# x loaded first, stage changes that wait for the last block but one, compression weights behind the modulation tiles, query rotation in the loop's first steps

## What is computed

```
c_act = silu(c)
mods  = c_act @ ada_w[l] + ada_b[l]            # shift, scale, gate of each norm ("modulation")
x = x + gate * hgrn2(modulate(rms_norm(x)))                    # segments h_q h_f h_v h_g h_out
x = x + gate * swiglu(modulate(rms_norm(x)))                   # ffn0_in / ffn0_out, twice
k, v = compress / select / window of modulate(rms_norm(x))     # n_kvc n_ks n_vs n_kw n_vw
q = rms_norm(per head)(modulate(x) @ w_q); q_rope = rope(q)    # n_q
x = x + gate * attention(q, q_rope, k, v) @ w_out              # attention loop, n_out
x = x + gate * swiglu(...)                                     # ffn1
x = x + diff_attention(rms_norm(x)) @ w_o                      # d_q d_k d_v d_out
x = x + squared_relu_mlp(rms_norm(x))                          # mlp0
x = x + s5(rms_norm(x)); x = x + squared_relu_mlp(...)         # s_glu, mlp1
```

## Time and profile before

| | value |
|---|---|
| median of three runs | 2970.71 us |
| profiled execution, its own time | 2976.58 us |
| its span in the trace | 2974.8 us |
| TensorE busy | 2788.4 us (94%) |
| VectorE busy | 1643.8 us (55%) |
| ScalarE busy | 1059.9 us (36%) |
| mean granted TensorE clock | 0.971 of full |

### The profile page before, as it was taken

One profiled execution on the slowest core, in us unless ns is written; L12 is line 12 of the kernel. 1 busy time (PEld: TensorE's weight loads), 2 busy tenths in 40 slices (PEclk: granted clock), 3 DMA queues, 4 the chain that ended last, 5 costly groups with the idle time before them and its releaser, 6 DMA issues.

```text
span 2974.8 us, 38309 instructions
## 1 busy us (share of the span) xinstructions
PE 2788.4 (94%) x14746; PEld 2238.9 (75%) x14746; DVE 1643.8 (55%) x2350; ACT 1059.9 (36%) x1559; POOL 100.4 (3%) x135
## 2 busy tenths in 40 slices
PE   5999999999979899999999998899999968999999
PEld 4898778888668556788887775788887757778787
DVE  4566566766436776533334557477777394353342
ACT  3312233222323565332233448332341524342231
POOL 2004000000011000000000100000000000000000
PEclk9999999999989999999999999999999988999999
DMA  5640346565363100333333420144444661323232
GB/s 209 199 148 1 105 136 198 149 197 157 105 182 107 43 1 15 97 88 96 94 87 110 126 79 1 57 101 134 141 143 150 231 108 64 92 85 99 85 99 71
DMA packets 402088, 326.36 MB, mean 110 GB/s; under 512 B 14920, under 2 KB 387360, under 8 KB 400928
## 3 DMA queue, kind: packets, MB, share of 16 engines
q1 hardware_dynamic: 319936, 232.80, 26.7%
q10 hardware_dynamic: 77376, 80.07, 8.4%
q0 software_dynamic: 4640, 11.60, 1.5%
HBM read 293.05 MB, written 19.86 MB: 105 GB/s over the span
## 4 chain that ended last, share of the span: by engine, by line
PE 62%; issue 23%; DVE 9%; DMA 3%; ACT 2%; POOL 1%; ACTq 1%; DVEq 0%; POOLq 0%
PE ps L451 44%; PE ps L429 3%; PE ps L445 2%; PE ps L433 1%; DVE ada_acc L1781 1%; DMA ada_ring<-in_ada_w 1%; PE ps L899 1%; DVE ada_ring L513 1%; PE ps L919 1%; PE ps L1649 1%; PE ps L2648 1%; PE ps L887 1%; DVE h_area L1783 1%; DVE h_area L1785 1%; DMA xin<-in_x 1%
## 5 line engine op out<-in xcount | busy, mean ns | idle before, releaser
L451 PE MATMUL ps<-hh,whi 128*128 128x512 f32 x1744 | 693.5, 398 | 5.0 <-DVE xT L2484 1.6
L451 PE MATMUL ps<-hh,wlo 128*128 128x512 f32 x1744 | 681.7, 391 | 0.0
L451 PE MATMUL ps<-hl,whi 128*128 128x512 f32 x1744 | 681.1, 391 | 0.0
L392 DVE TENSOR_TENSOR wlo<-raw,whi 128x2048 fp32r<-128x2048 f32 x198 | 453.9, 2292 | 364.7 <-ACT whi L388 364.7
L388 ACT ACTIVATE whi<-raw 128x2048 fp32r<-128x2048 f32 x198 | 377.6, 1907 | 381.5 <-PE ps L451 250.9
L451 PEld LDWEIGHTS ps<-hh,whi 128*128 128x128 f32 x1744 | 329.1, 189 | 80.0 <-issue 11.9
L451 PEld LDWEIGHTS ps<-hl,whi 128*128 128x128 f32 x1744 | 329.2, 189 | 71.6 <-issue 4.5
L451 PEld LDWEIGHTS ps<-hh,wlo 128*128 128x128 f32 x1744 | 328.8, 189 | 69.7
L451 PE MATMUL ps<-hid_h,whi 128*128 128x512 f32 x756 | 306.7, 406 | 0.0
L451 PE MATMUL ps<-hid_l,whi 128*128 128x512 f32 x756 | 298.4, 395 | 0.0
L451 PE MATMUL ps<-hid_h,wlo 128*128 128x512 f32 x756 | 298.4, 395 | 0.0
(11 more groups left out here) (413 smaller groups left out, 4076.0 us busy)
## 6 DMA issues: line engine op xcount, KB each, us to landing
raw<-in_ffn_w_in SPq DMA_DIRECT2D x44, 1024.0 KB, 6.0
ada_ring<-in_ada_w ACTq DMA_DIRECT2D x82, 512.0 KB, 4.4
raw<-in_ffn_w_up SPq DMA_DIRECT2D x32, 1024.0 KB, 5.3
raw<-in_ffn_w_down SPq DMA_DIRECT2D x32, 1024.0 KB, 5.6
raw<-in_ffn_w_out SPq DMA_DIRECT2D x32, 704.0 KB, 4.5
raw<-in_hgrn_w_in SPq DMA_DIRECT2D x16, 1024.0 KB, 5.6
raw<-in_attn_w_qkv SPq DMA_DIRECT2D x12, 1024.0 KB, 5.1
s_area<-cp_dram SPq DMA_DIRECT2D x6, 2048.0 KB, 9.0
```

What stands on the lines that cost most here:

```text
L392: nc.vector.tensor_tensor(wlo[:, par, :], raw[:, par, :], whi[:, par, :].bitcast(F32), ALU.subtract).then_inc(w_lo, 1)
L451: m = nc.tensor.matmul(ps[:, bank, :], tile(w, kt, j), x[:, kt, :], start=(kt == 0 and n == 0), stop=(kt == k - 1 and n == 2))
```

## The change

x is issued as the first DMA of SyncE's queue. Its squares are taken from the untransposed tiles (`accum_out` gives one sum per token), VectorE spreads the four sums over diagonal matrices, and four short matmuls with ones broadcast them. The folded sums are written in two groups, the scales in bank 4, then the shifts in bank 6, and VectorE adds the shifts (`first_shift`) behind the first two normed tiles, ahead of the first `convert_lo`. All changes of stage use the rule that `need` had. The compression weights are issued behind n_kvc's second block. In the last block of segments in `norm_after`, VectorE evicts ahead of `ada_sums`, and TensorE adds the squares ahead of the last `ada_products`. Query pair 1 moves from nb 8 to nb 9, pair 2 from nb 9 into loop steps 1 to 5, pair 3 from steps 4 to 8 into steps 6 to 10; the reciprocal roots get buffers of their own.

```diff
@@ sync
+            sp.dma_start(xin[:, :, :], a["x"][0].rearrange("(t p) d -> p t d", p=P)).then_inc(x_in, 16)
             for kt in range(FIRST):
@@ scalar
-            act.dma_start(xin[:, :, :], a["x"][0].rearrange("(t p) d -> p t d", p=P)).then_inc(x_in, 16)
...
             for kt in range(KT):
                 act.wait_ge(mm, kt + 1)
-                if kt >= 2:
-                    act.wait_ge(ssq_rdy, kt - 1)
-                nc.scalar.activation(sq[:, kt % 2, :], ps[:, kt % 4, :], ACT.Square).then_inc(sq_rdy, 1)
                 nc.scalar.activation(xT[:, kt, :], ps[:, kt % 4, :], ACT.Copy).then_inc(ev_v, 1)
+                if kt % 2:
+                    t = kt // 2
+                    if t >= 2:
+                        act.wait_ge(x_sq, t - 1)
+                    nc.scalar.activation((sq, xn)[t % 2][:, :, :].rearrange("p s n -> p (s n)"), xin[:, t, :], ACT.Square,
+                                         accum_out=x_ssq[:, t:t + 1]).then_inc(x_sq, 1)
@@ vector, ada_first_dve
+                if kt == 3:
+                    first_square_spread(dve)
+        def first_square_spread(dve):
+            for t in range(TT):
+                dve.wait_ge(x_sq, t + 1)
+                nc.vector.tensor_scalar(rstd[:, t * P:(t + 1) * P], ident[:, :], x_ssq[:, t:t + 1], None, ALU.mult
+                                        ).then_inc(sq_rdy, 2)
@@ tensor
+        def first_square_sums(pe):
+            for t in range(TT):
+                pe.wait_ge(sq_rdy, 2 * t + 2)
+                nc.tensor.matmul(ps[:, 7, t * P:(t + 1) * P], ones[:, :], rstd[:, t * P:(t + 1) * P], start=True, stop=True,
...
-            for j in range(NV):
...
-            m.then_inc(ada0_used, 1)
+            for bank, part in ((4, range(KT, NV)), (6, range(KT))):
...
+                m.then_inc(ada0_used, 1)
@@ scalar
+        def cmp_loads(act):
+            act.dma_start(w1v, a["cmp_w1"][1].rearrange("(m p) n -> p m n", p=P)).then_inc(w1_in, 16)
             act.dma_start(w1k, a["cmp_w1"][0].rearrange("(m p) n -> p m n", p=P)).then_inc(w1_in, 16)
...
         def n_hook_act(act, link, nb):
+            if nb == 1:
+                cmp_loads(act)
@@ vector
-            if nb >= 7:
-                for piece in query_pieces(dve, nb - 7):
+            if nb in (7, 9):
+                for piece in query_pieces(dve, (nb - 7) // 2):
...
-            last_query = query_pieces(dve, 3)
+            last_queries = query_pieces(dve, 2) + query_pieces(dve, 3)
...
-                if 4 <= w < 9:
-                    last_query[w - 4]()
+                if 1 <= w < 11:
+                    last_queries[w - 1]()
@@ vector, linear
+                    late = s.name in norm_after and isinstance(b, int) and b == s.n - 1
+                    if not late:
+                        ada_sums(dve, s, b, par)
                     evac(b, par)
+                    if late:
+                        ada_sums(dve, s, b, par)
@@ tensor, linear
-                if change and need is None:
-                    boundary(pe, s)
-                elif change:
+                if change:
                     if s.ea0 - prev.act > 0:
                         pe.wait_ge(ev_a, s.ea0 - prev.act)
                     pe.wait_ge(ev_v, s.ev0 - prev.dve)
...
-                ada_products(pe, s, s.n - 1, (s.g0 + s.n - 1) % 2)
                 if m is not None:
                     square_sums(s, m, s.n - 1, (s.g0 + s.n - 1) % 2)
+                ada_products(pe, s, s.n - 1, (s.g0 + s.n - 1) % 2)
```

More of the change, by code:

```diff
@@ L557, in ada_first_pe @@
             pe.wait_ge(ada0_sum_v, FIRST)
-            for j in range(NV):
-                m = nc.tensor.matmul(ps[:, 4, j:j + 1], ada_sum[:, j * P:j * P + P], ones[:, 0:1],
-                                     start=False, stop=True, skip_group_check=True)
-            m.then_inc(ada0_used, 1)
+            for bank, part in ((4, range(KT, NV)), (6, range(KT))):
+                for j in part:
+                    m = nc.tensor.matmul(ps[:, bank, j:j + 1], ada_sum[:, j * P:j * P + P], ones[:, 0:1],
+                                         start=(j == 0), stop=True, skip_group_check=True)
+                m.then_inc(ada0_used, 1)
         def ada_bias(dve, s):
@@ L2423, in _, with first_shift @@
             dve.wait_ge(cols_rdy, 1)
[L2424 to L2426 removed]
+            link(nc.vector.tensor_tensor(mods[:, 8:16], ps[:, 4, 8:16], cols_a[:, 8:16], ALU.add))
+            link(modulated_gain(0, ROWS["norm_mix"], 8))
+            def first_shift():
+                dve.wait_ge(ada0_used, FIRST + 2)
+                nc.vector.tensor_tensor(mods[:, 0:8], ps[:, 6, 0:8], cols_a[:, 0:8], ALU.add).then_inc(mods_rdy, 1)
                 convert_lo(dve, segs[0], 0, 0, 0)
@@ L2447, in apply @@
                                                    op0=ALU.mult, op1=ALU.mult).then_inc(xn_rdy, 1)
+                    if j == 0 and kt == 1:
+                        first_shift()
                     if kt:
@@ L2498, in _ @@
             if upto >= 2:
-                dve.wait_ge(mods_rdy, 1)
                 apply(0, 0, *mod_cols(0), FIRST_UNITS)
@@ L2675, in body @@
                     first = isinstance(b, int) and b == 0
-                    if change and need is not None and isinstance(b, int) and b == 1:
+                    if change and isinstance(b, int) and b == 1:
                         boundary(pe, s)
```

61 lines of the change are left out of this document (29 added, 32 removed).

## The result

The changed kernel takes 2947.27 us in the median of four executions (2944.24 to 2949.64), against 2973.28 us for the kernel before beside it (2970.0 to 2978.29): a ratio of 0.9911 with a 95% interval of 0.9892 to 0.9929, that is 26 us less. Its profiled execution took 2947.76 us, its span is 2945.8 us; the span before was 2974.8, so by the two traces the gain is 29.0 us. I had forecast 2931.7 us and 39.0 us of gain, with a range of 2921 to 2943: the gain was forecast too large by half, and the median lies 4 us above the range.

The account below looks back on a forecast made before the run. TensorE, busy 2788.4 of 2974.8 us, was taken as the bound, so only its waits and half clock could give much. Terms -17.3 - 16.2 - 6.5 - 1.9 + 2.9 = -39.0 from 2970.71 gave 2931.7 us, range 2921 to 2943.

Parts of the forecast that it names:

- start: Kernel start: first weight product at 39.7 instead of 57.04, -17.3 us, range -13 to -20.
- stage changes outside n_: At h_v, ffn0_in1, ffn1_in1, mlp1_in1: waits two blocks back are long met; part of -6.5 us, bounds 0 and -8.
- compression weights, with n_vs and n_vw: n_kvc to n_kw: loads moved behind let n_ks start earlier, -16.2 us; n_vs and n_vw waits also go.
- late eviction: Last blocks of h_out and n_out: eviction ahead of the sums, -1.9 us, bounds 0 and -2.5.
- query rotation: Attention loop: carries ten pieces instead of five, +2.9 us; 0 if hidden, +5.7 if nothing is hidden.
- I charge 1.0: Ahead of n_kw: weights ready between 856.4 and 863.4, n_vs covering TensorE until 861.4; 1.0 us charged.
- first rival: n_kw: ScalarE held too long by 4.4 MB of compression weights, TensorE waits 5.9 us plus 2.9 half clock; 2939.5, chance 0.15.
- The first modulation tile: n_kvc: tile issued at 823.6 instead of 836.87, landed at 830.4 instead of 844.2; n_ks starts 14.3 us earlier.
- third rival: Kernel start: the change does nothing, since DMA bounds it in any case; 2949.0 us, chance 0.05.
- second rival: Stage changes: waits only put off to the next block by late eviction or conversion; 2938.2 us, chance 0.08.
- slower rhythm: Attention loop: ten pieces push VectorE behind the exponentials, each of 68 steps keeps a longer turn; 3006 us, chance 0.02.
- signs of being wrong: L530 ending past 34, or ScalarE's L680 issues reaching past n_vs's end, with a gap ahead of n_kw's L451.

Follow-up runs that it names:

- the second trace: The changed kernel run once more without any further change, against the kernel before: 2943.53 us, ratio 0.9898.
- the last version: Changed kernel, old query rotation, tables behind n_kvc's second eviction, SyncE issuing compression loads behind n_kw's weights, w1v behind n_vw's: 2935.16 us, ratio 0.9862.
- the version in two parts: Changed kernel with compression loads split on ScalarE's queue, w1v one block later than the other four: 2943.47 us.

## Why the prediction was wrong, by its own steps

**The size.** Forecast were 39.0 us; the medians show 26.0 in one session and 31.3 in another; the two traces of the changed kernel stand 29.0 and 34.7 us under the one before. Term by term:

| term | forecast | changed kernel's trace |
|---|---|---|
| start | -17.3 | -16.4 |
| stage changes outside n_: h_v, ffn0_in1, ffn1_in1, mlp1_in1 | -4.0 | -4.7 |
| compression weights, with n_vs and n_vw | -16.2 - 2.5 = -18.7 | -13.8 (-12.8 again) |
| late eviction | -1.9 | -1.8 |
| query rotation | +2.9 | +3.2 |
| s5 and diff attention | 0 | +4.9 (-0.6 again) |

The terms themselves make -33.5 where I had -39.0: 5.5 us, of which 4.9 are in one stage. The rest of the 15.6 us between 2947.27 and 2931.7 is no term's: 4.9 are jumps in s5 and diff attention, 2.6 are the median of before, 2970.71 then and 2973.28 now, and 3.0 lie between the difference of two traces and that of the medians, less 0.4 that the trace shows beyond the terms. With the terms as they came out and nothing else, the time would have been 2937.2, within the range: the stage explains the largest error of the working, chance and the base carried the result out of the range.

**The step that failed** is in the term for the compression weights: "begun at 840.5 they hold ScalarE to 850 to 857", and "I charge 1.0". Moved by the 20.3 us that the stage now starts earlier, ScalarE came free at 862.3. The five issues held it for 24.8 us (26.1 in the second trace), where I had allowed 9.5 to 16.5. I had taken their duration from the earlier trace rows, 13.3 us, where the DMA view shows no bytes but those of ScalarE's own queue. I had named n_kw's weights and GpSimd's sixteen copies as company and added 3.2 us at most for them. The copies held back show what they cost: without them the hold is 15.0. The copies wait for n_kvc's second modulation product, and before they started at 852.97, 16 us behind the last of the issues; now they start at 819.82, 2.6 us behind the first. With the loads alone moved it is the same, a hold of 24.5 us, so the collision comes with the moved loads and does not need the stage's earlier start. It cost 0.6 to 1.8 us ahead of the head sums and 2.3 ahead of n_kw. My first rival named this mechanism, and its times were right: ScalarE free at 862, n_kw's weights at 868.4 (869.0 by n_kw's first product). It priced the wait at 5.9 + 2.9 us (of the 7.0 us between 861.4 and 868.4 it leaves 1.1 without a reason; the head sums stand there, 1.3 us). The waits were 2.9, with no half clock behind them, because n_ks started later and ran longer than worked out, and so n_vs covered TensorE to 864.1. The rival's chance of 0.15 was too low.

**The first modulation tile** came 1 us later than worked out (811.10, with 810.1 expected in this trace's time). The forecast took 5.1 us for the bytes and 1.5 us "to be seen"; no row or run shows the 1.5, and what the trace shows is 7.8 us from the issue at 803.27 to VectorE's first sum. So n_ks started 1.3 us late. I had also counted all of the 2.9 us of half clock as won, on the ground that the 9.8 us of idleness went; 2.08 us were left, TensorE fell to half clock behind them for 3.45 us, and the block gave back 1.3 of the 2.9. The Trainium skill ("TensorE: Matmul & The Clock Gate", "What's actually happening") says that activity releases the throttle. The trace agrees: the clock came back under unbroken work, and in the last version, where there is no wait, the 2.9 us are there. The length of the wait alone does not decide whether the clock falls: 2.00 us with the copies held back and 2.28 us ahead of n_kw in the changed kernel were followed by full clock.

By place, then, the 4.9 us of the stage are 1.3 for n_ks's start, 1.6 for its block, and 2.6 for the late waits (0.6 and 2.3, and head sums that took 0.7 us longer, less the 1.0 charged), less 0.6 that n_kw's and n_vw's blocks gained besides. They are not three causes that add. n_kw's first product is set by the chain behind ScalarE's hold, which starts with n_kvc's last eviction (817.11) and not with the modulation tile. By these rows an earlier tile alone would only have made the wait ahead of n_kw longer; that was not run. Without the hold's excess, with the copies held back, the stage comes to what was forecast, though the tile is as late there.

**Wrong in the parts.** I had charged 16.2 us to the moved loads and 2.5 to the moved waits of n_vs and n_vw. Alone they give 1.2 and 4.2; with both it is 11.6, and 12.8 to 13.8 in the changed kernel. My text said it ("n_vs covers TensorE until 861.4"), but did not see that this cover exists only by the other part.

**The base.** The forecast subtracts from 2970.71, the median of three executions; seven to twenty-one executions in later sessions gave 2974.39 to 2974.82. From there the same terms make 2935.6. I had allowed the median 2 us. The changed kernel's own medians, 2947.27 and 2943.53, differ by 3.7, and s5 alone took 285.5 to 291.5 us in the fourteen traces.

**What held.** The start: the first L429 near 40 (40.61), the fold at half clock (granted 0.50); the third rival is out. L530's fifth addition came at 24.54, later than the 23.5 that I had named as the limit, but behind it VectorE still waited 0.80 us for load 7, so nothing was lost by that. The Trainium skill ("DMA: Bandwidth & Descriptors", "Issuing engines are not separate DMA queues") spoke against a gain by bytes, and there is none, load 7 landing 1.0 us later than before; the 16.4 us are TensorE's work taken from behind the last byte, as worked out. The stage changes were gone and nothing came in their place, so the second rival is out. The loop cost 3.2 us (2.9 forecast) at the steps named, and did not lock into a slower rhythm. Of the signs of being wrong, the gap ahead of n_kw's L451 came (2.28 us), though the L680 issues ended at 839.53, ahead of n_vs's end at 843.8.

**Open.** Why the granted clock comes out at 0.76 or 0.86 in the same 36 us of s5; which of the trace's jumps in the loop of the version in two parts belong to it; and why the medians' gains, 26.0 and 31.3 us in two sessions, both stay below the 33.5 of the terms. And each run has one trace, so that its terms of 1 to 2 us are of the size by which h_out jumps.

## What to carry over

Find the lead at each stage's first product and follow it through the kernel: it separates what a change does from what chance does, which the total cannot; but take a second trace, to see what jumps by itself. A DMA issue occupies the engine that issues it for as long as its queue takes to accept it (0.37 us here with nothing in front, 18.16 for two behind 4 MB); before moving loads, ask what will share the DMA engines at the new place, counting what your own gain brings forward, and try large loads on the queue of an engine that nobody waits for (SyncE here), behind the weights that are wanted next. Price parts that act on the same stall together: a wait removed ahead of a held engine only moves to the next rule that asks for it.

## What I had not expected of the hardware

- Five DMA issues of 4.4 MB held ScalarE for 13.3 us when only its own queue moved bytes, 15.0 beside n_kw's weights, 24.8 beside those and sixteen copies of 128 KB within the SBUF; of these 18.16 us were two issues of 64 KB behind two of 2 MB.
- 2.08 us of idleness of TensorE were followed by 3.45 us at half clock; 1.07, 2.00 and 2.28 us at other places were not.
- In the same code, with the same busy time, a 36 us stretch had a granted clock of 0.76 in some executions and 0.86 in others, worth some 3 us.
